# RWKV chunk inverse: the second factor turned by VectorE in 32x32 blocks instead of multiplied, kept in the opposite half of the partitions

## The reference

```python
def step(S, inp):
    r_t, w_t, k_t, v_t, kk_t, b_t = inp
    sa = jnp.einsum('bhvk,bhk->bhv', S, kk_t)
    S = (S * w_t[:, :, None, :] - sa[..., None] * b_t[:, :, None, :]
         + v_t[..., None] * k_t[:, :, None, :])
    return S, jnp.einsum('bhvk,bhk->bhv', S, r_t)
```

## Time and profile before

| | |
|---|---|
| median of 3 runs | 2665.49 us |
| the profiled execution | 2672.74 us |
| its span, first to last instruction | 2671.0 us |
| mean granted TensorE clock | 0.97 of 2.4 GHz |
| the loop's chunks 0 to 11 | 1819.3 to 2138.4 us of the span |
| busy: PE, weight loads, DVE, ACT, POOL | 2488.5, 1925.8, 1335.5, 512.6, 141.3 us |

### The profile page before, as it was taken

The page is one execution under the profiler, slowest core; times in us unless marked ns, Lnnn a source line. Parts: engine busy times, 40 slices in busy tenths (PEclk is TensorE's granted clock), DMA queues, the critical chain, the costliest instruction groups (busy, mean ns, idle before and its releaser), DMA issues.

```text
span 2671.0 us, 49291 instructions
## 1 busy us (share of the span) xinstructions
PE 2488.5 (93%) x21560; PEld 1925.8 (72%) x21560; DVE 1335.5 (50%) x2478; ACT 512.6 (19%) x1032; POOL 141.3 (5%) x106
## 2 busy tenths in 40 slices
PE   8989999999999999999998989988887798999997
PEld 5945888888686548888884755457777746888786
DVE  4535555533454336555432365545665436787533
ACT  2122100101003320100001043323343222212100
POOL 0000000000000000000000000003223200000000
PEclk9988999999999999999999989998999998999998
DMA  5323322233221023222235102100000023222132
GB/s 165 119 79 126 95 71 88 75 87 107 64 66 62 1 77 113 95 79 70 77 93 160 48 16 66 51 1 4 5 4 4 4 95 119 71 95 95 48 88 71
DMA packets 221181, 190.53 MB, mean 71 GB/s; under 512 B 8727, under 2 KB 219064, under 8 KB 220968
## 3 DMA queue, kind: packets, MB, share of 16 engines
q1 hardware_dynamic: 220674, 187.29, 22.8%
q10 hardware_dynamic: 294, 0.09, 0.0%
HBM read 185.25 MB, written 2.10 MB: 70 GB/s over the span
## 4 chain that ended last, share of the span: by engine, by line
PE 86%; DVE 5%; issue 4%; ACT 1%; SPq 1%; POOL 1%; DMA 1%; DVEq 0%; POOLq 0%; ACTq 0%
PE psum L1630 30%; PE psum L1840 14%; PE psum L512 9%; PE psum L1130 4%; PE psum L2680 4%; PE psum L1344 3%; PE psum L2673 3%; PE psum L1341 3%; PE psum L3237 2%; PE psum L542 2%; PE psum L1066 1%; PE psum L2270 1%; PE psum L2252 1%; PE psum L1109 1%; PE psum L534 1%
## 5 line engine op out<-in xcount | busy, mean ns | idle before, releaser
L1630 PE MATMUL psum<-sbuf 128*128 128x256 f32 x3696 | 804.3, 381 | 4.0 <-DVE sbuf L476 1.9
L1630 PEld LDWEIGHTS psum<-sbuf 128*128 128x128 f32 x3696 | 704.7, 191 | 103.3 <-issue 3.2
L1840 PE MATMUL psum<-sbuf 128*128 128x256 f32 x1848 | 405.2, 382 | 11.1 <-DVE sbuf L1858 5.5
L1840 PEld LDWEIGHTS psum<-sbuf 128*128 128x128 f32 x1848 | 353.8, 192 | 62.1 <-DVE sbuf L1858 6.3
L1714 DVE TENSOR_TENSOR sbuf<-sbuf,psum 128x256 f32<-128x256 f32 x462 | 177.9, 417 | 200.5 <-PE psum L1630 199.3
L512 PE MATMUL psum<-sbuf 128*128 128x512 f32 (+3 forms) x688 | 248.1, 519 | 4.3 <-DVEq L617 4.0
L2680 PE MATMUL psum<-sbuf 64*64 64x64 f32 x4992 | 196.6, 225 | 40.3 <-issue 24.7
L512 PEld LDWEIGHTS psum<-sbuf 128*128 128x128 f32 (+2 forms) x688 | 129.6, 190 | 115.6 <-issue 103.4
L2680 PEld LDWEIGHTS psum<-sbuf 64*64 64x64 f32 x4992 | 170.6, 136 | 52.8 <-issue 43.9
L2673 PE MATMUL psum<-sbuf 64*64 64x64 f32 (+1 forms) x4544 | 176.1, 229 | 24.1 <-issue 17.9
L2673 PEld LDWEIGHTS psum<-sbuf 64*64 64x64 f32 x4544 | 158.6, 137 | 30.7 <-issue 21.5
(11 more groups left out here) (280 smaller groups left out, 2684.7 us busy)
## 6 DMA issues: line engine op xcount, KB each, us to landing
sbuf<-in_w_mod_dram SPq DMA_DIRECT2D x24, 1024.0 KB, 5.2
sbuf<-in_w_ffn_gate_dram SPq DMA_DIRECT2D x22, 1024.0 KB, 5.5
sbuf<-in_w_ffn_up_dram SPq DMA_DIRECT2D x22, 1024.0 KB, 7.6
sbuf<-in_w_ffn_down_dram SPq DMA_DIRECT2D x32, 704.0 KB, 6.0
sbuf<-in_w_up_dram SPq DMA_DIRECT2D x22, 1024.0 KB, 7.2
sbuf<-in_w_out_dram SPq DMA_DIRECT2D x12, 1024.0 KB, 8.1
sbuf<-in_w_in_dram SPq DMA_DIRECT2D x12, 1024.0 KB, 5.5
sbuf<-in_w_down_dram SPq DMA_DIRECT2D x16, 704.0 KB, 6.1
```

Source lines behind the costliest of these rows:

```text
L1630: mm = pe.matmul(bank, w[:, q, :], rhs[:, q, :], start=q == 0, stop=q == 3)
L1840: mm = pe.matmul(bank_of(g, p), wt[:, q, :], rhs_of[p][:, q, :], start=q == 0, stop=q == UNITS - 1)
```

## The change

X is no longer multiplied. The inverse lives in the half of the partitions opposite to its head's, and X is made from Y by VectorE's `transpose`, which turns each 32x32 block in its place (`turn_y`, a 128x256 tile per direction). Up to the last level the blocks that X needs are 32 or smaller, so whole 64x64 turns aren't needed.

- `gram_l`, `gram_lt`, x_init and X's product in `xy_level` are gone. The Gram matrices of B come crosswise into bank 6, 64 wide; in main chunks a second by_head product, 64 wide, goes to bank 7.
- T is computed crosswise into bank 2d, and ScalarE copies it back in two instructions, one for each half of the partitions. Y's product, by_head, goes to bank 2d + 1.
- VectorE: `update` subtracts 128x256 from Y, waits for itself, and turns. In level 3: GB's part 0, update and turn 0, y_init, in main chunks GB's part 1 (`gb_out`), update and turn 1. In level 4: products if any, both evacuations of GK, the wait for the identity, both first turns of the next chunk, then the two updates.
- TensorE: gram of K, an aside of level 4's t, waits for y_init and, in main chunks, for gb_out. Each t waits for `x_done`, the turn.
- GpSimd: LOFF of level 0 first, then the identity on Y alone (128x512 instead of 128x1024), then in even rounds the wait for both products, then LOFF of levels 1 to 4.

```diff
@@ -2702,7 +2702,7 @@
 ...
     sems = {n: k.sem(f"rwkv_{n}") for n in (
-        "latent_done", "rated", "cums_done", "exps", "k_gain", "kka", "k_made", "prods", "gram_l", "gram_lt", "gram_b", "gram_k", "x_init", "y_init",
+        "latent_done", "rated", "cums_done", "exps", "k_gain", "kka", "k_made", "prods", "gram_b", "gb_out", "gram_k", "y_init", "x_done",
         "gb", "gk", "loff", "eye", "t_done", "t_copied", "xy_done", "xy", "turned", "tok_copied", "kv_done", "kv_copied",
 ...
@@ -2781,35 +2781,26 @@
 ...
-        def gram_l(g):
-            wait("prods", prep(g // 2, 1))
-            if g == 1:
-                wait("gk", 1)
-            elif g >= 2:
-                wait("tok_copied", 3 * (g - 2) + 3)
+        def gram(g, tile, signal):
+            if tile is K:
+                wait("y_init", g + 1)
+                if main(g):
+                    wait("gb_out", g - NCH_CTX + 1)
+            else:
+                wait("prods", prep(g // 2, 1))
+                if g == 1:
+                    wait("gk", 1)
+                elif g >= 2:
+                    wait("tok_copied", 3 * (g - 2) + 3)
             for p in range(8):
-                mm = by_head(pe, k.bank[7][:, column(p)], feature(AR, g, p // 4, p % 4)[:, 0, :], feature(B, g, p // 4, p % 4))
-                if p == 7:
-                    mm.then_inc(sems["gram_l"], 1)
-                yield
-
-        def gram_lt(g):
-            if g >= 2:
-                wait("tok_copied", 3 * (g - 2) + 2)
-            for p in range(8):
-                mm = crosswise(pe, k.bank[6][:, column(p)], feature(B, g, p // 4, p % 4), feature(AR, g, p // 4, p % 4)[:, 0, :])
-            mm.then_inc(sems["gram_lt"], 1)
-
-        def gram(g, tile, signal):
-            if tile is B:
-                wait("y_init", g + 1)
-            else:
-                wait("gb", g + 1)
-            for p in range(8):
-                rhs = feature(AR, g, p // 4, p % 4)
-                rhs = flat(rhs) if main(g) else rhs[:, 0, :]
+                x, rhs = feature(tile, g, p // 4, p % 4), feature(AR, g, p // 4, p % 4)
                 o = (p % 4) * P
-                mm = by_head(pe, k.bank[6 + p // 4][:, o:o + (P if main(g) else CH)], feature(tile, g, p // 4, p % 4), rhs)
+                if tile is K:
+                    mm = by_head(pe, k.bank[6 + p // 4][:, o:o + (P if main(g) else CH)], x, flat(rhs) if main(g) else rhs[:, 0, :])
+                else:
+                    mm = crosswise(pe, k.bank[6][:, column(p)], x, rhs[:, 0, :])
+                    if main(g):
+                        mm = by_head(pe, k.bank[7][:, column(p)], x, rhs[:, 1, :])
                 if p == 7:
 ...
@@ -2839,11 +2830,7 @@
 ...
                     wait("loff", LEVELS * n + lv + 1)
-                if lv == 0:
-                    if d == 0:
-                        wait("eye", n + 1)
-                else:
-                    wait("xy", halves(n, lv - 1, d))
+                wait("x_done", halves(n, lv, d))
                 if lv == 0 and n >= 1:
 ...
@@ -2856,9 +2843,7 @@
 ...
                 for p in range(4 * d, 4 * d + 4):
-                    if lv < LEVELS - 1:
-                        crosswise(pe, k.bank[2 * d + 1][:, column(p % 4)], Y[n % 2][:, p, :], T[:, p, :])
-                    mm = by_head(pe, k.bank[2 * d][:, column(4 + p % 4)], T[:, p, :], Y[n % 2][:, p, :])
+                    mm = by_head(pe, k.bank[2 * d + 1][:, column(p % 4)], T[:, p, :], Y[n % 2][:, p, :])
                 mm.then_inc(sems["xy_done"], 1)
 ...
@@ -2925,9 +2910,7 @@
 ...
                 aside = nothing
-                if lv == 1 and g < NCH:
-                    aside = gram_l(g)
-                elif lv == 2 and m >= 0:
+                if lv == 2 and m >= 0:
                     aside = outputs(m)
 ...
@@ -2953,8 +2936,6 @@
 ...
                     xy_level(n, lv)
-                if lv == 1 and g < NCH:
-                    gram_lt(g)
                 if lv == 2 and 0 <= m < NCH - 1:
 ...
@@ -2997,7 +2978,9 @@
 ...
                         wait("t_done", halves(n, lv, d))
-                        act.activation(flat(T[:, half(d), :]), k.bank[2 * d][:, 0:256], ACT.Copy).then_inc(sems["t_copied"], 1)
+                        for h, o in zip(HEADS, HEADS[::-1]):
+                            ins = act.activation(flat(T[o, half(d), :]), k.bank[2 * d][h, 0:256], ACT.Copy)
+                        ins.then_inc(sems["t_copied"], 1)
                 if lv == 0:
 ...
@@ -3063,13 +3046,16 @@
 ...
-        def x_init(g):
-            wait("gram_l", g + 1)
-            dve.tensor_tensor(split(X[g % 2]), k.bank[7].rearrange("p (d f t) -> p d f t", d=2, f=4), both("x1", CH),
-                              ALU.mult).then_inc(sems["x_init"], 1)
-            wait("gram_lt", g + 1)
-            dve.tensor_tensor(split(Y[g % 2]), k.bank[6].rearrange("p (d f t) -> p d f t", d=2, f=4), both("y1", CH),
-                              ALU.mult).then_inc(sems["y_init"], 1)
+        def y_init(g):
+            dve.tensor_tensor(split(Y[g % 2]), k.bank[6].rearrange("p (d f t) -> p d f t", d=2, f=4), both("y1", CH), ALU.mult).then_inc(sems["y_init"], 1)
+
+        def turn_y(n, d):
+            dve.transpose(flat(X[n % 2][:, half(d), :]), flat(Y[n % 2][:, half(d), :])).then_inc(sems["x_done"], 1)
+
+        def evacuate_b(g, part):
+            mask_ = mask(k, "gram", part * CH, 7 * CH).rearrange("p (x w) -> p x w", w=CH)[:, 0::4, :].unsqueeze(2).broadcast_to([P, 2, 4, CH])
+            src_ = k.bank[6 + part].rearrange("p (d f t) -> p d f t", d=2, f=4)
+            return dve.tensor_tensor(split(GB[g % 2][:, :, part, :]), src_, mask_, ALU.mult)
 ...
@@ -3079,11 +3065,11 @@
 ...
             wait("xy_done", halves(n, lv, d))
-            w = 2 if lv < LEVELS - 1 else 1
-            xy = XY[n % 2][:, 0:w, half(d), :].rearrange("p w f t -> p w (f t)")
-            o = 1024 * d + 256
-            new = k.psum[:, o:o + 256 * w].rearrange("p (w t) -> p w t", w=w)
-            dve.tensor_tensor(xy, xy, new, ALU.subtract).then_inc(sems["xy"], 1)
+            y = flat(Y[n % 2][:, half(d), :])
+            dve.tensor_tensor(y, y, k.bank[2 * d + 1][:, 0:256], ALU.subtract).then_inc(sems["xy"], 1)
+            if lv < LEVELS - 1:
+                wait("xy", halves(n, lv, d))
+                turn_y(n, d)
 ...
@@ -3103,26 +3089,28 @@
 ...
             for lv in range(LEVELS):
+                if lv == 3 and g < NCH:
+                    wait("gram_b", g + 1)
+                    evacuate_b(g, 0).then_inc(sems["gb"], 1)
                 if lv == 4 and exps_in(n) is not None:
                     products(exps_in(n), 0)
-                if lv == 3 and g < NCH:
-                    wait("gram_b", g + 1)
-                    evacuate(g, GB, 0, 0)
                 if lv == 4 and g < NCH:
 ...
                     evacuate(g, GK, 0, 1)
+                    evacuate(g, GK, 1, 1).then_inc(sems["gk"], 1)
+                    wait("eye", g + 1)
+                    for d in range(2):
+                        turn_y(g, d)
                 if live:
 ...
                 if lv == 3 and g < NCH:
-                    evacuate(g, GB, 1, 0).then_inc(sems["gb"], 1)
-                if lv == 4 and g < NCH:
-                    evacuate(g, GK, 1, 1).then_inc(sems["gk"], 1)
+                    y_init(g)
+                    if main(g):
+                        evacuate_b(g, 1).then_inc(sems["gb_out"], 1)
                 if live:
 ...
                     rate_products(exps_in(n))
-                if lv == 1 and g < NCH:
-                    x_init(g)
                 if lv == 1 and exps_in(n) is not None:
 ...
@@ -3150,15 +3138,13 @@
 ...
             if g < NCH:
-                wait("x_init", g + 1)
+                loff(g, 0)
                 wait("y_init", g + 1)
+                pool.tensor_tensor(Y[g % 2], Y[g % 2], mask(k, "eye", 0, CH).unsqueeze(1).broadcast_to([P, 8, CH]), ALU.add).then_inc(
+                    sems["eye"], 1)
                 if exps_in(n) is not None:
-                    wait("k_made", prep(exps_in(n), 1))
-                xy = XY[g % 2].rearrange("p w a t -> p (w a) t")
-                pool.tensor_tensor(xy, xy, mask(k, "eye", 0, CH).unsqueeze(1).broadcast_to([P, 16, CH]), ALU.add).then_inc(sems["eye"], 1)
-                for lv in range(LEVELS):
-                    if lv in (0, 2) and exps_in(n) is not None:
-                        wait("prods", prep(exps_in(n), lv // 2))
+                    wait("prods", prep(exps_in(n), 1))
+                for lv in range(1, LEVELS):
                     loff(g, lv)
 ...
```

## The result

The changed kernel takes **2651.66 us**, the median of 6 runs (2650.14 to 2655.53), against 2665.57 for the kernel before on the same chip: a ratio of 0.9945, with a 95% interval of 0.9931 to 0.9960, that is 11 to 18 us. Run again beside other kernels it gave 0.9938 (0.9924 to 0.9952). It is faster, inside the range, by about 15 us where 23 were forecast. The two profiled executions, 2672.74 and 2650.34 us, happen to differ by 22.4.

The account below looks back on a forecast made before the run. The loop was taken as bound by TensorE's instruction count where dense, by the chain of engines where sparse. 319 - 57 + 18 + 20 gives 300, -19, and -4 ahead of it: -23, 2642.5 us; range 2612 to 2667.

Parts of the forecast that it names:

- The mechanism: RWKV loop: TensorE's gaps are code loading, one per 128 weight loads, 3.75 to 3.95 us a block; 16 of 85 go.
- loading by count: TensorE in the loop: gaps follow the number of instructions, one per 128 weight loads with their matmuls.
- array work: TensorE in the loop: gaps come from the array's work or time, so dropping instructions alone gains nothing.
- Rival 3: Loop: gaps are not of loading by count, the 57 us stay, only added work counts; +14, 2679.5 us; chance 0.10.
- The turn: VectorE's transpose making X from Y, 128x256 per direction, taken at 0.42 us.
- Rival 2: VectorE's turns are dear: 2662 us at 0.69 us each, 2704 at 1.28; chance 0.12.
- The levels: Loop chunks: each level's added cost, from -0.2 at even chunks' level 0 to +1.5 at even main chunks' level 4.
- The stalls' size: TensorE's gaps in the loop: 57 us, the middle of 46.2 at matmuls and 69.1 at weight loads, 20 remaining.
- what stays: TensorE's gaps left in the loop after the change: mean 1.65 us a chunk, 20 us over 12 chunks.
- the chain: Loop: serial work added by turns, copies and level 4, +1.0 to +2.3 us a chunk, taken as +18 in all.
- Ahead of the loop: Before the loop's first level: gram_l and gram_lt leave a serial chain that nothing hides, -4 us.
- Rival 1: Loop: the added 18 us hide in waits that the next block's loading needs anyway; 2624 us; chance 0.15.

Follow-up runs that it names:

- experiments 1: Changed kernel with an unread product of 4 columns put where X's product stood, restoring the instruction count: 2673.46 us, ratio 1.0020 to the kernel before.
- experiment 2: Kernel before, without X's product in levels 0 to 3 and zeros in the banks VectorE reads for it: 2630.26 us, ratio 0.9870.
- experiment 3: Changed kernel with T copied by one 128x256 ScalarE instruction instead of two 64x256 ones: 2645.4 us, ratio 0.9916.
- edit 5: Changed kernel with y_init and GB's second part moved ahead of update 0 in level 3, where VectorE idled: 2640.73 us, ratio 0.9904.
- experiment 4: Changed kernel with each turn made twice, the second behind the first: 2695.87 us, ratio 1.0115.
- experiment 6: Changed kernel with y_init and GB's second part ahead of update 0, and even rounds' products moved out of level 4's way: 2635.35 us, ratio 0.9888.

## Why the prediction was right, and where it was off

**The mechanism held.** Gaps once per 128 loads, 68 packets, a half-level of Y still 0.46 us, X's product worth nothing to the array: experiments 1 and 2 came out at 2673 and 2630 us, where loading by count said 2673 and 2630 and array work said 2652 and 2665. Rival 3 has fallen: leaving out 1,536 loads and matmuls that took the array next to no time gave 35 us. The rule of the Trainium skill (Runtime: NRT & Kernel Launch, Instruction fetch mechanics) that the fetch is hidden doesn't hold in this loop, where TensorE issues 64x64 products.

**The turn** was put at 0.42 us and took 0.44. The estimate of 0.62, twice the 311 ns of the Trainium skill (VectorE: DVE Perf Modes, The three transpose paths), was too high. Rival 2 is out. Update and turn together take 0.89 us in the rows above (2039.79 to 2040.68), for the 0.87 worked out.

**The levels**, compared where no gap falls into them: level 0 of even chunks takes 4.52 us for 4.77 (put at -0.2), level 3 4.86 for 4.73 (+0.18). Level 4 was put at +0.6 in odd and +1.5 in even main chunks and is +0.8 and +1.65. In chunks 0 to 3 it was put at +0.3 and is +1.30, +0.24, +1.31 and +0.80, 2.4 us more over the four. ScalarE's pair takes 0.77 us, not 0.66, and by experiment 3 opened 0.30 us at level 2 of main chunks for the 0.25 put down and 0.47 in the others for 0.7, 4.3 us in all.

**The stalls' size is the term that was off.** The step took 57 us, the middle between the matmuls' 46 and the weight loads' 69, as what would vanish without gaps. With 20 left, the term was -37. Neither view moved by that much: at the matmuls "issue" fell from 46.2 to 11.8 us, -34.4, at the weight loads from 69.1 to 36.4, -32.7. By the matmuls' view the start had been put 11 us too high and what stays 8 us too high; that most of the two errors cancels is luck. With -34 for the stalls, the chain comes to about +19 by difference, for +18. That +19 was not measured by itself: between experiment 2 and the changed kernel the loop grows by 17.4 us, a difference that also holds the Gram matrices and what gaps and clock did. The loop: -15.5 measured, -19 forecast.

**Ahead of the loop** -4.2 were measured for -4, and then chunk 0 gave 2.9 back (23.0 us for 20.2), which no step had. Two things lie in it. Level 4 of chunk 0 takes 5.45 us for 4.15 with the clock at full speed in both kernels, so that part is the chain. The other is the clock. In the changed kernel, chunk 0's first 7 us, then around level 4 of chunk 3 (columns as in the earlier trace rows, the clock third from the end):

```profile
1812.55:1819.50 6.95, 6.58 (x122) 6.23 (x122) 3.61 (x8) 3.96 (x10) 2.47 (x3) 0.50 0.01 2
1904.71:1906.00 1.29, 0.42 (x8) 0.34 (x12) 1.29 (x3) 0.32 (x1) 0.76 (x1) 0.93 0.00 0
1906.00:1909.30 3.30, 3.30 (x60) 3.19 (x60) 0.54 (x2) 0.82 (x3) 3.30 (x4) 0.51 0.02 5
```

In the second trace of the kernel before, chunk 0's first 3 us and the next 12:

```profile
1813.64:1816.60 2.96, 2.96 (x84) 2.96 (x86) 0.06 (x1) 1.76 (x4) 1.21 (x1) 0.50 0.02 6
1817.60:1830.00 12.40, 10.72 (x465) 9.76 (x461) 9.79 (x18) 5.33 (x11) 2.36 (x1) 1.00 0.02 4
```

TensorE's clock before the loop is 0.50, 1.2 GHz, in both. The changed kernel came to chunk 0 4 us earlier and stayed at 1.2 GHz for 7 us of it, the other for 3. With edit 5, whose trace had the clock back at the start of level 1, that level took 4.04 us; in the changed kernel it took 5.08. So the clock is about 1 of the 2.9 us.

**What is open.** Loop and start give -19.7 us, the medians -14 and -16. Most of the difference has a place, ahead of the loop, in code that is the same in both kernels. It is a stretch of the attention's products (L2252 and on), shown here between the same two weight loads, first in the second trace of the kernel before, then in the changed kernel, columns as in the earlier trace rows:

```profile
1549.86:1568.50 18.64, 16.48 (x59) 8.89 (x58) 15.14 (x31) 10.03 (x19) 0.00 (x0) 0.82 0.00 0
1550.48:1571.46 20.98, 19.98 (x58) 10.13 (x57) 15.14 (x31) 10.03 (x19) 0.00 (x0) 0.67 0.00 0
```

It takes 18.64 us in both traces of the kernel before and in that of experiment 2, and 20.9 to 21.3 at a clock of 0.67 or 0.68 in all seven traces of the changed kernel and its variants. With smaller differences around it, the stretch from 1405 to 1622 us takes 216.3 us in the three and 219.6 to 220.6 in the seven. So 3 to 4 us of what loop and start gained are lost there to a longer stay at 1.2 GHz. Why a change 200 us later in the program should do this, no run shows. The first 180 us differ by 5 us between the two traces of the kernel before, which is the rest of the spread. Rival 1, an added chain that hides under the loading, is true in small part only: in experiment 4 nearly each added turn was paid, and the loading gave back 8 of some 38 us.

## What to carry to other kernels

Where TensorE issues small products back to back, count its instructions: a gap "issue" after each 128 weight loads with a packet of 16 KB in the instruction queue says that a product which the array takes for nothing costs its place in the stream. Before replacing it, look at where VectorE idles; here the same edit was worth 15 us with the new work between two updates and 24 with it in the idle time ahead of them (29 with the products moved as well). A replacement for a hidden product costs most on the chain of a level where engines already wait for each other, here level 4.

## What the runs showed of the hardware that I had not expected

- Dips of the granted clock inside the loop. In the rows above, 1904.71 to 1906.00 TensorE's matmuls were busy 0.42 of 1.29 us, waiting for gram_k's evacuations; then the clock was 0.51 for 3.3 us and level 4 of chunk 3 took 7.2 us instead of 5.6. There are two such dips in the loop of the changed kernel's first trace and three in its second, none in either trace of the kernel before, one with X's product left out, 14 with each turn twice. They come at other places in each execution, so the wait shown is not proven to be what starts one.
- Two 64x256 copies of ScalarE take 0.77 us, a step of 0.39, where two of 128x256 take 0.66 with a step of 0.28: half the partitions, and no shorter.
- A product of VectorE from SBUF to SBUF (128x512) that meets a mask of GpSimd of that size took up to 1.76 us instead of 0.68, and the mask 1.73 instead of 1.27 (experiment 6).
